# A transformer-like pair of blocks on one core: the first projections read the input before its norm, and matmuls await the low part of their weights by quarters

## The chip, the cores and the metric

The kernel runs on one core of a Trainium2 chip, all in float32. The metric is the device time of one execution in microseconds (us), the median of several runs. TensorE is called PE here, VectorE DVE, ScalarE ACT, GpSimd POOL and SyncE SP, as in the profile.

## The reference, cut to what matters

Only the beginning of the first block matters for the first half of the change.

```python
def rms_norm(x, g):
    y = x * lax.rsqrt(jnp.mean(x * x, axis=-1, keepdims=True) + EPS)
    return y * g
...
h = rms_norm(x, mix_norm_g[l])              # x: 1024 tokens x 1024 channels
p = jnp.einsum("btd,de->bte", h, w_in[l])
(gm_u, gm_v, cv_a, cv_g, dn_q, dn_k, dn_v, dn_g, dn_beta, dn_alpha) = jnp.split(p, offsets, axis=-1)
y_a = spatial_gating(jax.nn.gelu(gm_u), jax.nn.gelu(gm_v), ...)   # gm_u, gm_v: 256 channels each
```

The factor `rsqrt(mean(x*x) + EPS)` belongs to a token, not to a channel. So it can also be multiplied into the result of the projection. After this come a convolution branch, a gated delta rule, an output projection, a SwiGLU (`ffn0`), and a second block (`ffn1`, attention with a state-space part and a gated linear unit `glu`, `ffn2`), each with its norms.

## The kernel before, in words

Activations lie transposed: 128 channels on the partitions, tokens along the free dimension, so `x[:, k, :]` is the k-th of 8 groups of channels. The 1024 tokens are worked on as two chunks of 512 columns, c = 0 and c = 1.

Each float32 product is three matmuls on rounded halves: both operands are split into a high part (`w_hi`, `h_hi`, rounded to the type `fp32r`) and a low part (`w_lo`, `h_lo`, the rest), and hi·hi, hi·lo and lo·hi are summed in a PSUM bank of `acc`. For the weights this goes as a pipeline over *slabs*. A slab is one output tile of 128 channels with all its k-tiles (`kt`, mostly 8). SP loads it to `w_raw[:, j]`, ACT copies it rounded to `w_hi[:, j]` (`w_high`), POOL subtracts to get `w_lo[:, j]` in four pieces of a quarter each (`split`, L558; each adds 1 to `split_done`), and PE runs `pe_slab`: 3 matmuls for each k and chunk, so 24 for a chunk of 8 k-tiles. There are two buffers, j = 0 and j = 1, and 368 slabs in all; a *pair* is one of each. SP reloads a `w_raw` buffer when its four pieces are done; ACT overwrites `w_hi[:, j]` when PE has finished the slab before in that buffer.

`slab_plan` lists the slabs as segments (`gm`, `cv`, `dn_kv`, ...). The first pair or so of a segment is written out, the others run in a hardware loop (`pe.Fori`), in which the number that a semaphore is compared with is computed in a register. Some segments are marked `fine`: in their written-out slabs PE awaits the quarter of `w_lo` that the next k needs. All other slabs, those in loops among them, await all four pieces before their first matmul (L675).

At the start ACT squares `x` (L622), PE sums the squares over the channels with a matrix of 1/1024 (L605, 16 matmuls of full float32), ACT takes the root (L627), DVE the reciprocal (L651), and DVE, ACT and POOL make `h = x*g*rs` and its halves (L661, L632, L665, L593), first for chunk 0 and then for chunk 1. PE begins with the 8 small outputs `logits` (L1155 to L1157) and the first pair of `gm` for chunk 0, and does the same for chunk 1. ACT applies Gelu from the bank to `gm_u` and `gm_v` (L1406, L1429). Then come the `cv` slabs. The order on each engine is that of the code.

Of the kernel before, what the change touches and what calls it, by code (L numbers as in the profile page):

```python
# [132 lines left out]
def slab_plan(t):  # L133
# [62 lines left out]
    add("gm", 2, KD, CH1, run(t["w_in"], 0))  # L196
# [84 lines left out]
def build_program(nc, t):  # L281
    with ExitStack() as ctx:
# [54 lines left out]
        sqx = place("sqx", W + 8 * col, [P, 2, L])  # L337
# [149 lines left out]

        @block.sync
# [60 lines left out]
        def _(pool):  # L549

            for name, seg in LOADED.items():
# [9 lines left out]
                if name not in ("gm", "out1a"):  # L561
# [6 lines left out]
                if name == "out1a":  # L568
                    pool.wait_ge(sem("x_kept"), 32)
                    pool.memset(xn[0:DB, :, DB:2 * DB], 0.0).then_inc(sem("xn_zero"), 1)  # L570
                    def mix_low(k, src):
                        pool.wait_ge(sem("mix_hi"), k + 1)
                        pool.tensor_tensor(h_lo[:, k, META:L], src, h_hi[:, k, META:L].bitcast(F32), ALU.subtract).then_inc(sem("o_lo"), 1)

                    for k in range(2):
                        mix_low(k, gm_u2[:, k, :])
                    for p in range(2):
                        pool.wait_ge(sem("o_scaled"), 2 * p + 2)
                        for hd in range(HEADS):
# [10 lines left out]
                for c, (c0, w) in enumerate(seg.chunks):  # L590
                    for k in POOL_LO if name == "gm" else ():
                        pool.wait_ge(sem("hi_mix1"), c * KD + k + 1)
                        pool.tensor_tensor(h_lo[:, k, c0:c0 + w], tmp[:, k % 4, 0:w], h_hi[:, k, c0:c0 + w].bitcast(F32),  # L593
                                           ALU.subtract).then_inc(sem("lo_written"), 1)
# [5 lines left out]
        def pe_first_norm(pe):  # L600

            for c, (c0, w) in enumerate(CH1):
                for k in range(KD):
                    pe.wait_ge(sem("sqt_mix1"), c * KD + k + 1)
                    ins = pe.matmul(acc[:, c, 0:w], const("mean"), sqx[:, k % 2, c0:c0 + w],  # L605
                                    start=(k == 0), stop=(k == KD - 1), skip_group_check=True)
                    ins.then_inc(sem("sqsum_mix1"), 1)

        def act_first_norm(act):

            for g in range(4):
                c, k = g // 2, 4 * (g % 2)
                c0, w = CH1[c]
                act.dma_start(x[:, k:k + 4, c0:c0 + w], t["x"][:, k:k + 4, c0 - META:c0 - META + w]).then_inc(sem(f"x_full{g}"), 16)

            def square(c, k):
                c0, w = CH1[c]
                if k % 4 == 0:
                    act.wait_ge(sem(f"x_full{2 * c + k // 4}"), 16)
                if k >= 2:  # L620
                    act.wait_ge(sem("sqsum_mix1"), c * KD + k - 1)
                act.activation(sqx[:, k % 2, c0:c0 + w], x[:, k, c0:c0 + w], ACT.Square).then_inc(sem("sqt_mix1"), 1)  # L622

            def root(c):
                c0, w = CH1[c]
                act.wait_ge(sem("sqsum_mix1"), (c + 1) * KD)
                act.activation(rs[:, c0:c0 + w], acc[:, c, 0:w], ACT.Sqrt, bias=const("eps")).then_inc(sem("sd_mix1"), 1)  # L627

            def high(c, k):
                c0, w = CH1[c]  # L630
                act.wait_ge(sem("scaled_mix1"), c * KD + k + 1)
                act.copy(h_hi[:, k, c0:c0 + w], tmp[:, k % 4, 0:w]).then_inc(sem("hi_mix1"), 1)  # L632

            act.wait_ge(sem("params_full"), 32)
            for k in range(KD):
                square(0, k)
            root(0)
            for j in range(2):
# [8 lines left out]
        def dve_norm(dve, own, name, chunks, gain):

            for c, (c0, w) in enumerate(chunks):
                dve.wait_ge(sem("sd_" + name), c + 1)  # L650
                own.link(dve.reciprocal(rs[:, c0:c0 + w], rs[:, c0:c0 + w]))  # L651
                for k in range(KD + 2):
                    if k < KD:
                        g = c * KD + k
                        if g >= 4:
                            before = (k - 4) % KD
                            if before in POOL_LO:
                                dve.wait_ge(sem("lo_written"), (g - 4) // KD * len(POOL_LO) + POOL_LO.index(before) + 1)
                            else:
                                own.wait()  # L660
                        dve.scalar_tensor_tensor(tmp[:, k % 4, 0:w], x[:, k, c0:c0 + w], gain[:, k:k + 1],  # L661
                                                 rs[:, c0:c0 + w], ALU.mult, ALU.mult).then_inc(sem("scaled_" + name), 1)
                    if k >= 2 and k - 2 not in POOL_LO:
                        dve.wait_ge(sem("hi_" + name), c * KD + k - 1)
                        own.mark(dve.tensor_tensor(h_lo[:, k - 2, c0:c0 + w], tmp[:, (k - 2) % 4, 0:w],  # L665
                                                   h_hi[:, k - 2, c0:c0 + w].bitcast(F32), ALU.subtract))
                own.wait()
                dve.sem_inc(sem("h_written"), 1)

        def pe_slab(pe, seg, i, j, rhs, only=None, late=None):  # L670

            n = len(seg.chunks)
            fine = seg.fine and isinstance(i, int) and only is None
            if not fine:
                pe.wait_ge(split_done, i * (2 * LOW_PIECES) + LOW_PIECES * (seg.n0 + j + 1))  # L675
            for c, (c0, w) in enumerate(seg.chunks):
# [7 lines left out]
                for k in range(seg.kt):  # L684
# [5 lines left out]
                    rh, rl = rhs[0][:, k, c0:c0 + w], rhs[1][:, k, c0:c0 + w]  # L690
# [191 lines left out]

        def pe_first_pair(pe, seg, beside):

            for c in range(len(seg.chunks)):
                h_ready(pe, c)
                beside(c)
                for j in range(2):
                    pe_slab(pe, seg, 0, j, (h_hi, h_lo), only=c)
# [254 lines left out]
        def pe_mix1(pe):  # L1144
            h = (h_hi, h_lo)

            def logits_chunk(c):

                if c == 0:
                    pe.wait_ge(sem("ba_full"), 1)  # L1150
                name = f"logits_{c}"
                aux_take(pe, name)
                out, cols = aux(name)[0:8, :], slice(META + 512 * c, META + 512 * (c + 1))
                for k in range(KD):
                    pe.matmul(out, ba_hi[:, k, :], h_hi[:, k, cols], start=(k == 0), stop=False)  # L1155
# [11 lines left out]
            for j in range(2):  # L1167
                pe_slab(pe, SEG["gm"], 1, j, h)
# [231 lines left out]
        def act_mix1(act):  # L1400
# [3 lines left out]
            def first_pair(j, c):  # L1404
# [1258 lines left out]
```

## Time and profile before

| | us |
|---|---|
| median of 3 runs | 3679.59 (3678.3 to 3680.5) |
| the profiled execution, its own time | 3681.67 |
| its span (first to last instruction) | 3679.9 |
| PE busy | 3562.0 (97%) |
| DVE, ACT, POOL busy | 1440.2, 958.7, 1129.1 |
| mean granted TensorE clock | 0.985 |

The span is what the trace covers; the own time is 1.8 us more. The durations below come from this execution, the forecast is made against the median, 2.1 us below its own time. A clock of 1.00 is TensorE's higher level, 2.4 GHz, and 0.50 the lower, 1.2 GHz.

### The profile page before, as it was taken

To read this page: it belongs to the slowest core of one execution; us is meant where nothing else is said; L and a number is where in the kernel's file an instruction comes from. 1 tells how busy PE (TensorE), PEld (TensorE's weight loads), DVE (VectorE), ACT (ScalarE), POOL (GpSimd) and SP (SyncE) were. 2 spreads that over 40 slices of the span, in tenths; PEclk is the share of its full clock that TensorE was granted. 3 is DMA by queue.
4 is the path that set the end of the run, shared out by engine and by line. 5 is a ranking of instruction groups with operands and counts; after the bars stand their busy time and mean duration, and the time that the engine had idled before them with its cause. 6 is when DMAs were issued, how large, how long until landed. Compare 5 with 4: busy or idle time off the path is not lost.

```text
span 3679.9 us, 52405 instructions
## 1 busy us (share of the span) xinstructions
PE 3562.0 (97%) x20104; PEld 2947.3 (80%) x20104; DVE 1440.2 (39%) x2514; ACT 958.7 (26%) x1678; POOL 1129.1 (31%) x1503
## 2 busy tenths in 40 slices
PE   7998889999999999999999989999999999999998
PEld 4787777888888878899999878887777788888886
DVE  3297455211111163412122473836876521111214
ACT  4244443111111142111111233115653321111112
POOL 3242135322222253222222442301015532222223
PEclk9999899999999999999999999999999999999999
DMA  2111112111111121111111232111024221111112
GB/s 99 47 46 41 51 69 86 60 49 46 46 49 48 42 79 56 42 46 43 49 42 54 59 123 86 35 36 38 30 90 143 86 68 47 46 46 52 46 44 99
DMA packets 79299, 217.45 MB, mean 59 GB/s; under 512 B 18848, under 2 KB 18976, under 8 KB 78496
## 3 DMA queue, kind: packets, MB, share of 16 engines
q1 hardware_dynamic: 60960, 171.25, 15.1%
q10 hardware_dynamic: 18176, 43.93, 3.3%
q8 instruction: 114, 1.87, 0.2%
q14 instruction: 49, 0.40, 0.0%
HBM read 194.62 MB, written 19.46 MB: 58 GB/s over the span
## 4 chain that ended last, share of the span: by engine, by line
issue 61%; POOL 24%; PE 11%; DVE 2%; ACT 1%; DMA 1%; POOLq 1%; SPq 0%; ACTq 0%; DVEq 0%
POOL w_lo L558 23%; PE acc L691 2%; PE acc L692 2%; PE acc L693 2%; PE acc L1225 0%; POOLq L562 0%; DVE cv_acc L1700 0%; PE acc L1220 0%; DVE acc L1778 0%; DVE x_up L1781 0%; PE acc L605 0%; PE acc L1339 0%; DMA x<-in_x_dram 0%; PE acc L1282 0%; PE acc L1312 0%
## 5 line engine op out<-in xcount | busy, mean ns | idle before, releaser
L558 POOL TENSOR_TENSOR w_lo<-w_raw,w_hi 128x256 fp32r<-128x256 f32 (+3 forms) x1472 | 1090.3, 773 | 2415.4 <-ACT w_hi L528 2415.1
L691 PE MATMUL acc<-h_hi,w_hi 128*128 128x512 f32 (+1 forms) x3552 | 1318.4, 371 | 27.5 <-POOL w_lo L558 19.9
L692 PE MATMUL acc<-h_lo,w_hi 128*128 128x512 f32 (+1 forms) x3552 | 1317.3, 371 | 0.0
L693 PE MATMUL acc<-h_hi,w_lo 128*128 128x512 f32 (+1 forms) x3552 | 1311.8, 369 | 0.0
L691 PEld LDWEIGHTS acc<-h_hi,w_hi 128*128 128x128 f32 x3552 | 672.2, 189 | 156.6 <-issue 20.5
L692 PEld LDWEIGHTS acc<-h_lo,w_hi 128*128 128x128 f32 x3552 | 671.4, 189 | 120.0 <-issue 1.9
L693 PEld LDWEIGHTS acc<-h_hi,w_lo 128*128 128x128 f32 x3552 | 672.3, 189 | 117.0
L528 ACT CAST w_hi<-w_raw 128x1024 fp32r<-128x1024 f32 (+3 forms) x368 | 344.1, 936 | 1242.4 <-PE acc L693 1230.7
L971 DVE TENSOR_TENSOR ff_hi<-tmp,acc 128x512 f32 (+3 forms) x154 | 94.5, 614 | 1100.5 <-PE acc L693 1065.0
L691 PE MATMUL acc<-ff_hi,w_hi 128*128 128x512 f32 (+1 forms) x1232 | 449.4, 365 | 5.4 <-POOL w_lo L558 2.9
L693 PE MATMUL acc<-ff_hi,w_lo 128*128 128x512 f32 (+1 forms) x1232 | 447.1, 363 | 0.0
L692 PE MATMUL acc<-ff_lo,w_hi 128*128 128x512 f32 (+1 forms) x1232 | 446.6, 362 | 0.0
L1009 DVE SCALAR_TENSOR_TENSOR x<-acc,x 128x512 f32 (+1 forms) x168 | 103.3, 617 | 440.8 <-PE acc L693 439.6
L691 PEld LDWEIGHTS acc<-ff_hi,w_hi 128*128 128x128 f32 x1232 | 231.8, 188 | 52.3 <-issue 6.7
L693 PEld LDWEIGHTS acc<-ff_hi,w_lo 128*128 128x128 f32 x1232 | 231.6, 188 | 38.0
L692 PEld LDWEIGHTS acc<-ff_lo,w_hi 128*128 128x128 f32 x1232 | 231.3, 188 | 38.2 <-issue 0.7
L938 ACT ACTIVATE tmp<-acc 128x512 f32<-128x512 f32 (+1 forms) x136 | 72.9, 537 | 532.8 <-PE acc L693 532.6
L976 DVE TENSOR_TENSOR ff_lo<-tmp,ff_hi 128x512 f32 (+3 forms) x154 | 113.9, 740 | 23.0 <-DVE tmp L973 20.7
L842 DVE SCALAR_TENSOR_TENSOR x<-acc,x 128x512 f32<-128x512 f32 (+1 forms) x88 | 56.6, 643 | 165.4 <-PE acc L693 160.2
L973 DVE TENSOR_TENSOR tmp<-tmp,acc 128x512 f32<-128x512 f32 (+1 forms) x154 | 93.4, 606 | 0.0
L1700 DVE SCALAR_TENSOR_TENSOR cv_acc<-cv_y,params,cv_acc 128x1024 f32<-128x1024 f32 x60 | 80.5, 1388 | 0.0
L2257 ACT ACTIVATE sc<-sc,st 128x272 f32<-128x272 f32 (+1 forms) x128 | 64.0, 500 | 32.1 <-DVE st L2504 29.1
(361 smaller groups left out, 2978.0 us busy)
## 6 DMA issues: line engine op xcount, KB each, us to landing
w_raw<-in_ffn_w_dram SPq DMA_DIRECT2D x94, 512.0 KB, 3.5
w_raw<-in_w_in_dram SPq DMA_DIRECT2D x58, 512.0 KB, 3.5
w_raw<-in_w_out_dram SPq DMA_DIRECT2D x32, 512.0 KB, 3.5
w_raw<-in_ffn_w_dram SPq DMA_DIRECT2D x48, 320.0 KB, 2.9
w_raw<-in_w_gate_dram SPq DMA_DIRECT2D x24, 512.0 KB, 3.5
w_raw<-in_w_up_dram SPq DMA_DIRECT2D x24, 512.0 KB, 3.5
w_raw<-in_ffn_w_dram SPq DMA_DIRECT2D x32, 384.0 KB, 3.0
gates_kept<-gstage ACTq DMA_DIRECT2D x32, 256.0 KB, 2.0
```

Of the source, the lines that this page charges most:

```text
L528: act.copy(w_hi[:, j, 0:width], w_raw[:, j, 0:width]).then_inc(sem("w_high"), 1)
L558: pool.tensor_tensor(w_lo[:, j, a:a + step], w_raw[:, j, a:a + step], w_hi[:, j, a:a + step].bitcast(F32), ALU.subtract).then_inc(split_do ...
L691: pe.matmul(bank, wh, rh, start=(k == 0), stop=False)
L692: pe.matmul(bank, wh, rl, start=False, stop=False)
L693: ins = pe.matmul(bank, wl, rh, start=False, stop=(k == seg.kt - 1))
L938: act.activation(tmp[:, c, 0:w], acc[:, c, 0:w], ACT.Silu).then_inc(acc_free[0], 1)
L971: own.mark(dve.tensor_tensor(hi, g, up, ALU.mult))
L973: dve.tensor_tensor(tmp[:, 3:4, 0:w], g, up, ALU.mult).then_inc(acc_free[1], 1)
L976: own.mark(dve.tensor_tensor(ff_lo[:, bass.ds(f, 1), c0:c0 + w], tmp[:, 3:4, 0:w], hi.bitcast(F32), ALU.subtract))
L1009: dve.scalar_tensor_tensor(xt, acc[:, 3 * j + c:3 * j + c + 1, 0:w], scale, xt, ALU.mult, ALU.add).then_inc(acc_free[j], 1)
L1700: own.mark(dve.scalar_tensor_tensor(cv_acc[:, ct, :], src, w, cv_acc[:, ct, :], ALU.mult, ALU.add))
L2257: own.mark(act.activation(probs(u, hd), probs(u, hd), ACT.Exp, bias=st[0:nq, b, 0, hd:hd + 1], accum_out=st[0:nq, b, 1, hd:hd + 1]))
```

## The change

1. The slabs of `gm` are cut up in another way. `gm_a` is both pairs for chunk 0, on `hx = x*g` without the norm's factor. `gm_r` runs the second pair again for chunk 1 with the weights that are still there, and `gm_b` loads the first pair again for chunk 1, both on `h` with the norm. So two more slabs are loaded and split, and no matmul of theirs is done twice.
2. `hx` gets its own halves in tiles of its own (`hx_hi` by ACT, `hx_lo` by DVE). PE's 16 float32 matmuls for the sum of squares become one for each chunk, since DVE first adds the squares of the 8 k (`ssq0`). DVE multiplies the results of `gm_a` and of `logits` for chunk 0 by the factor `rs0`, and Gelu is then applied in place. All low parts of `h` are made by DVE and none by POOL, first for chunk 1, then for chunk 0.
3. `x` comes in six transfers and not four: parts of 0.5 MB on SP's and ACT's queues for chunk 0, then two of 1 MB. The constants are loaded behind the first weights.
4. `pe_slab` awaits quarters of `w_lo` in every slab, in loops too, except where it runs for one chunk alone (`only`).

```diff
-    add("gm", 2, KD, CH1, run(t["w_in"], 0))
+    add("gm_a", 2, KD, CH1[:1], run(t["w_in"], 0), lambda i, j, c: 3 * j + i)
+    add("gm_r", 1, KD, CH1[1:], None, lambda i, j, c: 3 * j + 2, again=True)
+    add("gm_b", 1, KD, CH1[1:], run(t["w_in"], 0), lambda i, j, c: 3 * j)
...
+        X_PARTS = [(0, 0, 2), (0, 2, 2), (0, 4, 2), (0, 6, 2), (1, 0, 4), (1, 4, 4)]
...
-            sp.dma_start(consts[:, :], t["consts"]).then_inc(sem("params_full"), 16)
             sp.dma_start(params[:, :], t["params"]).then_inc(sem("params_full"), 16)
...
                     for j in range(2):
+                        load_x(sp, 2 * j)
                         load(0, j)
+                    sp.dma_start(consts[:, :], t["consts"]).then_inc(sem("consts_full"), 16)
...
+        def pe_first_mean(pe, c):
+            pe.wait_ge(sem("x_added"), (KD - 1) * (c + 1))
+            pe.matmul(acc[:, 6 + c, :], const("mean"), ssq0[:, c, :], start=True, stop=True, skip_group_check=True)\
+              .then_inc(sem("x_ms"), 1)
...
+            for g in (1, 3, 4, 5):
+                load_x(act, g)
...
+            for k in range(KD):
+                raw_high(k)
+                if k % 4 == 3:
+                    w_high(act, SEG["gm_a"], 0, k // 4)
             for k in range(KD):
                 square(0, k)
+            w_after(act, SEG["gm_a"], 0, 0)
             for k in range(KD):
                 square(1, k)
+            act.wait_ge(sem("consts_full"), 16)
+            w_after(act, SEG["gm_a"], 0, 1)
+            for c in range(2):
+                root(c)
             for k in range(KD):
+                act_first_high(act, 1, k)
...
+        def dve_first_norm(dve, own):
+            for k in range(KD):
+                dve.wait_ge(sem("hx_hi_full"), k + 1)
+                dve.scalar_tensor_tensor(hx_lo[:, k, :], x[:, k, FIRST], gain[:, k:k + 1], hx_hi[:, k, :].bitcast(F32),
+                                         ALU.mult, ALU.subtract).then_inc(sem("hx_full"), 1)
+            for c in range(2):
+                for k in range(1, KD):
...
+                    dve.tensor_tensor(ssq0[:, c, :], ssq0[:, c, :], sq0[:, n % 3, :], ALU.add).then_inc(sem("x_added"), 1)
+            for c in range(2):
+                dve.wait_ge(sem("sd_mix1"), c + 1)
+                own.mark(dve.reciprocal(rs0[:, c, :], rs0[:, c, :]))
...
+            split(1)
+            for i in range(2):
+                for j in range(2):
+                    acc_wait(dve, SEG["gm_a"], i, j, 0)
+                    dve.tensor_tensor((gm_u, gm_v)[i][:, j, 0:512], acc[:, 3 * j + i, :], rs0[:, 0, :], ALU.mult).then_inc(acc_free[j], 1)
...
+            split(0)
...
-            fine = seg.fine and isinstance(i, int) and only is None
+            fine = only is None
...
+            pe_slab(pe, gm_a, 0, 0, hx, late=lambda c, k: pe.wait_ge(sem("hx_full"), k + 1), at=META)
+            pe_slab(pe, gm_a, 0, 1, hx, at=META)
+            pe.wait_ge(sem("consts_full"), 16)
+            pe_first_mean(pe, 0)
+            pe_slab(pe, gm_a, 1, 0, hx, late=lambda c, k: pe_first_mean(pe, 1) if k == 6 else None, at=META)
+            pe_slab(pe, gm_a, 1, 1, hx, at=META)
+            logits_chunk(0, hx, META)
+            pe_slab(pe, gm_r, 0, 0, h, late=lambda c, k: pe.wait_ge(sem("lo_mix1"), k + 1))
+            logits_chunk(1, h, 0)
+            pe_slab(pe, gm_r, 0, 1, h)
+            pe_slab(pe, gm_b, 0, 0, h)
...
-            for j in range(2):
-                pe_slab(pe, SEG["gm"], 1, j, h)
+            pe_slab(pe, gm_b, 0, 1, h)
+            pe.wait_ge(sem("lo_mix1"), 2 * KD)
             pe_slab(pe, SEG["cv"], 0, 0, h)
```

Here is how PE's own order begins. Before, the sums of squares stand ahead of the first product (`sqx` are the squares, `ba_hi` the weights of `logits`):

```order
L605 MATMUL acc<-sqx,consts 128x512 [waits sqt_mix1,params_full]
L605 MATMUL acc<-sqx,consts 128x512 [waits sqt_mix1] x15
```

After the change, PE's order begins with the first slab, which waits for a piece of `w_lo` and for one k of `hx_lo`:

```order
L725 MATMUL acc<-hx_hi,w_hi 128x512 [waits split_done,hx_full]
L726 MATMUL acc<-hx_lo,w_hi 128x512
L727 MATMUL acc<-hx_hi,w_lo 128x512
L725 MATMUL acc<-hx_hi,w_hi 128x512 [waits hx_full]
L726 MATMUL acc<-hx_lo,w_hi 128x512
L727 MATMUL acc<-hx_hi,w_lo 128x512
L725 MATMUL acc<-hx_hi,w_hi 128x512 [waits split_done,hx_full]
```

The 16 matmuls on squares have left PE's front, and weights stand there.

DVE's order after the change, behind the eight `hx_lo` (L667): the sums, both reciprocals, and the first splits of chunk 1, which PE's `gm_r` slab awaits one by one (`ssq_77`, `sq_75` and `rs_76` are `ssq0`, `sq0` and `rs0`):

```order
L667 SCALAR_TENSOR_TENSOR hx_lo<-x,params,hx_hi 128x512 [waits hx_hi_full] x7
L675 TENSOR_TENSOR ssq_77<-ssq_77,sq_75 128x512 [waits x_sq]
L675 TENSOR_TENSOR ssq_77<-ssq_77,sq_75 128x512 [waits x_added,x_sq] x13
L678 RECIPROCAL rs_76<-rs_76 128x512 [waits sd_mix1] x2
L687 SCALAR_TENSOR_TENSOR gm_u<-x,params,rs_76 128x512 [waits dve_own]
L687 SCALAR_TENSOR_TENSOR gm_u<-x,params,rs_76 128x512
L687 SCALAR_TENSOR_TENSOR gm_v<-x,params,rs_76 128x512
L691 TENSOR_TENSOR h_lo<-gm_u,h_hi 128x512 [waits hi_mix1]
```

Before, DVE had one reciprocal and then the splits of chunk 0, and POOL made most of the low parts; now both reciprocals stand ahead of the first split.

In a loop body (`ffn0`'s up projections, and all others alike) PE had this at the head of its first slab:

```order
L700 UNCONDITIONAL_BRANCH
L700 ISA
L680 ISA [waits split_done]
L691 MATMUL acc<-h_hi,w_hi 128x512 [waits acc_free0]
L692 MATMUL acc<-h_lo,w_hi 128x512
L693 MATMUL acc<-h_hi,w_lo 128x512
```

Now it has a register operation and a wait more for each further quarter:

```order
L722 ISA [waits acc_free0]
L725 MATMUL acc<-h_hi,w_hi 128x512 [waits split_done]
L726 MATMUL acc<-h_lo,w_hi 128x512
L727 MATMUL acc<-h_hi,w_lo 128x512
L725 MATMUL acc<-h_hi,w_hi 128x512
L726 MATMUL acc<-h_lo,w_hi 128x512
L727 MATMUL acc<-h_hi,w_lo 128x512
L722 REGISTER_ALU
L725 MATMUL acc<-h_hi,w_hi 128x512 [waits split_done]
```

The wait for the whole split has become one for its first piece, and three register operations with a wait each have come into each slab of a loop.

## Rows read from the trace of the kernel before

**Rows 1.** Whom PE waited for, over the span: total, times, longest.

```profile
PE acc L691 <- POOL w_lo L558: 25.7, 17, 5.3
PE acc L605 <- ACT sqx L622: 21.2, 5, 12.9
PE acc L1225 <- DVE dec_s L1721: 10.3, 4, 4.7
```

**Rows 2.** Busy time (instructions) of PE, PEld, DVE, ACT, POOL by stretch; PEclk, DMA share, GB/s.

```profile
16.00:42.00 26.00, 17.27 (x29) 5.16 (x27) 14.69 (x11) 16.44 (x26) 15.64 (x14) 0.84 0.23 74
42.00:99.50 57.50, 57.44 (x250) 41.28 (x251) 16.65 (x17) 22.14 (x33) 18.27 (x18) 0.98 0.13 42
```

**Rows 3.** Timeline of the first stage: start, duration, engine, line, operation.

```profile
0.76 6.65 ACTq L614 DMA_DIRECT2D x<-in_x_dram  x4
8.24 0.20 DVE L2594 CAST ba_hi<-params 128x64 fp32r<-128x64 f32 x1 [8.24 <-DMA params<-in_params_dram]
10.82 1.28 ACT L622 ACT_TABLE_LOAD   x1 [10.82 <-DMA x<-in_x_dram]
12.11 1.15 ACT L622 ACTIVATE sqx<-x 128x512 f32<-128x512 f32 x2
22.89 1.98 ACT L528 CAST w_hi<-w_raw 128x1024 fp32r<-128x1024 f32 x2
42.31 3.35 DVE L651 RECIPROCAL rs<-rs 128x512 f32<-128x512 f32 x1 [2.71 <-ACT rs L627]
99.46 0.60 ACT L1429 ACTIVATE gm_v<-acc 128x512 f32<-128x512 f32 x1 [4.96 <-PE acc L693]
```

**Rows 4.** Lines L661, L558, L665 in the first 60 us: ns min/median/max.

```profile
L661 DVE SCALAR_TENSOR_TENSOR tmp<-x,params,rs x16: 739/1061/1789, 26.4 to 55.2; 128x512 f32<-128x512 f32 x16
L558 POOL TENSOR_TENSOR w_lo<-w_raw,w_hi x8: 724/950/1180, 24.0 to 30.1; 128x256 fp32r<-128x256 f32 x8
L665 DVE TENSOR_TENSOR h_lo<-tmp,h_hi x4: 678/1218/1779, 34.2 to 55.8; 128x512 fp32r<-128x512 f32 x4
```

**Rows 5.** Lines near to the operations that are new, over the span.

```profile
L1686 DVE TENSOR_TENSOR gm_u<-gm_u,acc x4: 686/688/689, 164.1 to 170.2; 128x512 f32<-128x512 f32 x4
L712 PE MATMUL acc<-ssq,consts x22: 385/592/1061, 570.2 to 3666.0; 128*128 128x512 f32 x18, 128*128 128x264 f32 x4
```

**Rows 6.** Timeline behind the first stage, with what DVE's idle time was ended by.

```profile
114.40 0.43 DVE L1663 BATCH_NORM_STATS2 small<-gm_t 128x6 f32<-128x256 f32 x1 [28.47 <-ACT gm_t L1445]
```

**Rows 7.** PE at the first slab of `at_g`, and POOL's pieces for this pair.

```profile
2180.93 9.09 POOL L558 TENSOR_TENSOR w_lo<-w_raw,w_hi 128x256 fp32r<-128x256 f32 x8 [9.11 <-ACT w_hi L528]
2185.53 0.79 PE L691 MATMUL acc<-h_hi,w_hi 128*128 128x512 f32 x1 [3.58 <-POOL w_lo L558]
```

**Rows 8.** PE alone by stretch: busy (instructions), PEclk, DMA share, GB/s.

```profile
2185.50:2191.00 5.50, 5.47 (x13) 0.51 0.29 95
```

**Rows 9.** Whom PE waited for in the loop of `glu`, 2744 to 2830 us.

```profile
PE acc L691 <- POOL w_lo L558: 2.9, 3, 1.5
```

**Rows 10.** Timeline at a turn of that loop.

```profile
2746.97 0.39 PE L693 MATMUL acc<-y_hi,w_lo 128*128 128x512 f32 x1
2748.81 0.49 PE L691 MATMUL acc<-y_hi,w_hi 128*128 128x512 f32 x1 [1.46 <-POOL w_lo L558]
...
2751.46 0.39 PE L693 MATMUL acc<-y_hi,w_lo 128*128 128x512 f32 x1
2751.69 0.40 PE L691 MATMUL acc<-y_hi,w_hi 128*128 128x512 f32 x1
...
2754.47 0.40 PE L691 MATMUL acc<-y_hi,w_hi 128*128 128x512 f32 x1
```

**Rows 11.** PE's sequencer in loops: register operations and waits, ns min/median/max.

```profile
L680 PEldq ALU_OP  x109: 32/36/42, 707.0 to 3584.6; - x109
L680 PEldq EVENT_SEMAPHORE  x84: 51/51/51, 712.6 to 3590.3; - x84
```

**Rows 12.** Line L675 between 2748 and 2752 us: its register operation.

```profile
L675 PEldq ALU_OP  x1: 32/32/32, 2750.3 to 2750.3; - x1
```

More of the change, by code:

```diff
@@ L590, in _ @@
[L590 to L594, printed above, removed]
+                pool.wait_ge(sem("x_kept"), 32)
+                pool.memset(xn[0:DB, :, DB:2 * DB], 0.0).then_inc(sem("xn_zero"), 1)
@@ L597, in _, with first_stage @@
                         split(i, j)
[L600 to L607, printed above, removed]
-        def act_first_norm(act):
[L611 to L614, printed above, removed]
+        def first_stage(c, k):
+            return (gm_u, gm_v)[k % 4 // 2][:, k % 2, 512:1024] if c else tmp0[:, k % 4, :]
@@ L647, in dve_norm, with act_first_high @@
[L647 to L651, printed above, removed]
+                act_first_high(act, 1, k)
+        def act_first_high(act, c, k):
+            c0, w = CH1[c]
+            act.wait_ge(sem("scaled_mix1"), first_no(c, k) + 1)
+            act.copy(h_hi[:, k, c0:c0 + w], first_stage(c, k)).then_inc(sem("hi_mix1"), 1)
@@ L663, in dve_norm @@
[L663 to L670, printed above, removed]
+                        if k >= 4:
+                            dve.wait_ge(sem("lo_mix1"), first_no(c, k) - 3)
@@ L1402, in act_mix1, with second_gelu @@
             act.dma_start(gm_par[:, :], t["gm"]).then_inc(sem("gm_par_full"), 16)
-            def first_pair(j, c):
-                acc_wait(act, SEG["gm"], 0, j, c)
-                act.activation(gm_u[:, j, cc(c)], acc[:, 3 * j + c, :], ACT.Gelu).then_inc(acc_free[j], 1)
-            for c in range(2):
-                aux_wait(act, f"logits_{c}")
-                aux_release(act.copy(lgt[0:8, cc(c)], aux(f"logits_{c}")[0:8, :]), f"logits_{c}")
-                for j in range(2):
-                    if c:
-                        w_after(act, SEG["gm"], 0, j)
-                    first_pair(j, c)
+            def second_gelu(seg, tile, j):
+                acc_wait(act, seg, 0, j, 0)
+                act.activation(tile[:, j, 512:1024], acc[:, seg.bank(0, j, 0), :], ACT.Gelu).then_inc(acc_free[j], 1)
+            for i in range(2):
+                for j in range(2):
+                    act.wait_ge(acc_free[j], chunk_no(SEG["gm_a"], i, 0) + 1)
+                    dst = (gm_u, gm_v)[i][:, j, 0:512]
+                    own.mark(act.activation(dst, dst, ACT.Gelu))
+            for k in range(KD):
+                act_first_high(act, 0, k)
+                if k == 3:
+                    w_high(act, SEG["gm_b"], 0, 0)
+                    second_gelu(SEG["gm_r"], gm_v, 0)
+            aux_wait(act, "logits_1")
+            aux_release(act.copy(lgt[0:8, cc(1)], aux("logits_1")[0:8, :]), "logits_1")
+            second_gelu(SEG["gm_r"], gm_v, 1)
+            w_high(act, SEG["gm_b"], 0, 1)
+            own.wait()
+            for j in range(2):
+                act.wait_ge(acc_free[j], chunk_no(SEG["gm_r"], 0, 0) + 1)
+            act.sem_inc(sem("gm_full"), 8)
+            second_gelu(SEG["gm_b"], gm_u, 0)
+            w_after(act, SEG["gm_b"], 0, 0)
             aux_wait(act, "logits")
@@ L1425, in act_mix1 @@
             act.sem_inc(sem("z_ln_full"), 1)
-            for j in range(2):
-                for c in range(2):
-                    acc_wait(act, SEG["gm"], 1, j, c)
-                    act.activation(gm_v[:, j, cc(c)], acc[:, 3 * j + c, :], ACT.Gelu).then_inc(acc_free[j], 1)
-                w_after(act, SEG["gm"], 1, j)
-            for j in range(2):
-                act.wait_ge(acc_free[j], chunk_no(SEG["gm"], 1, 1) + 1)
-            act.sem_inc(sem("gm_full"), 8)
+            second_gelu(SEG["gm_b"], gm_u, 1)
+            w_after(act, SEG["gm_b"], 0, 1)
             for s in range(4):
```

142 lines of the change are left out of this document (70 added, 72 removed).

## The prediction, made before the kernel was run

> **What bounds the kernel now.** I first asked the page's table of busy times: PE works for 97% of the span, so a gain can only come out of the 3% in which it stands still, out of matmuls that go away, or out of a higher clock. Next came the list of whom PE waits for [rows 1]. It shows 21.2 us for the squares of the first norm, 25.7 us in 17 waits for the first low weights, and 10.3 us for DVE in the delta rule. Then I went to the places. At the start PE has 29 records in 16 to 42 us, halves of the full float32 sums, then 250 in 57.44 us at 0.230 us each, without a gap [rows 2]. The stage ends when ACT reads `gm_v`, at 99.46 [rows 3]. So the start is 42 us of preparation and 57.4 us of products. In the later pairs I looked at two kinds of wait for `w_lo`: at `at_g`, 3.58 us [rows 7], and in the loop of `glu`, 2.9 us in three [rows 9].
>
> **The start, step by step.** Removed: the norm of chunk 0 stands no longer ahead of the first product. What must still be there is `x`, its gain, and a piece of weights.
> - ACT's own queue issues `x` until 0.76 + 6.65 = 7.4; the table load of 1.28 follows, 8.7 [rows 3]. Before, ACT waited until 10.82, when its 1 MB part landed. Now the first part is 0.5 MB, on SP's queue behind parameters that landed at 8.24 even behind the constants, which now come later. So `x` is no longer last here, ACT's issue is.
> - Four casts to `hx_hi`, priced as squares of the same shape, 1.15 / 2 = 0.575 each: 11.0. Half a slab of `w_hi`, 1.98 / 2 = 0.99: 12.0 [rows 3]. POOL's first piece at its fastest, 0.72 [rows 4]: **PE begins at 12.7**, not at 42.0.
> - The products are the same 240, and 10 small ones, so 57.4 us if fed; two sums over channels take 0.6 each [rows 5]: 12.7 + 57.4 + 1.2 = 71.3.
> - PE then starts from rest. At `at_g`, 13 matmuls after a wait took 5.47 us at a granted clock of 0.51 [rows 8], the lower of the two levels, 2.5 more than 13 x 0.23. The old stretch has a clock of 0.98 over 57.5 us [rows 2], so about 1.2 of this is in it already: 1.3 more, 72.6. This also covers `hx_lo`, which DVE makes at 0.74 to 1.06 each [rows 4] while a k takes PE 3 x 0.42.
> - The critical hand-off is `gm_r`. PE has 120 matmuls ahead of it (four slabs and `logits`): 12.7 + 27.6 + 1.2 + 2.5 = 44.0. DVE must by then have done 8 `hx_lo`, 14 additions, two reciprocals and the first splits. The additions follow ACT's squares (8 x 0.575 for each chunk between casts of weights), and end at about 23 and 29. The second sum stands in PE's third slab at k = 6, at about 30.7; with a root behind it the reciprocals run from 31.4 to 38.1, 3.35 each [rows 3]. Three scalings go ahead of the first low part: 38.1 + 3 x 0.74 + 0.68 = 41.0, the next each 1.42 later [rows 4]. PE wants one each 0.69 from 44.0 on. The first five are early; k = 5 is there at 48.1 and wanted at 47.5, and the last two need no scaling, 48.8 and 49.5. That makes 0.6 of waiting; I take 0.9 with what a late root would add: **`cv` starts at 73.5, a gain of 26.0**.
> - Behind it: four products from the bank, 0.69 each [rows 5], to 52.3; then the split of chunk 0, 11.3 us undisturbed, 18.2 at the medians [rows 4], to 63.6 or 70.5. `cv` wants it at 73.5. It is hidden, with 3 us left at worst. The two further slabs cost ACT 2 us and POOL four pieces each (2.9 to 4.7) [rows 3, 4]. The first is wanted at 60.6 and its buffer is free at 49.5; the second is wanted at 66 and its buffer is free at 60.6, and by quarters it is 61.6 + 0.7 to 1.2. Both are hidden; with no cover each would cost 5 to 7.
> - The two ends: with no stall of any kind 71.3, a gain of 28.2. If DVE ran split and scalings at medians, 2.28 a pair for 1.42, the split of chunk 1 costs 6.9 more, and a reciprocal or root late by 1 adds to it: gain 18. I am near the good end, because POOL has nothing to split between 35 and 49: `gm_r` uses weights that are there, and the next slab's buffer is still held.
>
> DVE operations with both inputs in SBUF spread from 0.68 to 1.78 us here while POOL's pieces spread from 0.72 to 1.18 [rows 4], but the product that reads PSUM stays within 0.686 to 0.689 [rows 5]. The Trainium skill, GpSimd page ("Specifications"), states that GpSimd shares its SBUF interfaces with VectorE and contends with instructions of two SBUF inputs; by that rule alone a DVE chain beside four slabs of splitting would run at its medians and the gain be near 18, and by the rows, since POOL rests at that time, 26.
>
> **Does it last?** The later chain shifts with it if nothing there is tied to something other than PE. DVE is idle for 28.47 us before 114.40, waiting for ACT's Gelu behind PE's bank [rows 6], so it can go 26 earlier. Loads have room: the DMA share is 0.13 in the dense stretch [rows 2].
>
> **The quarter waits.** Most of the 25.7 us [rows 1] are in slabs that are already `fine` and wait for their first piece. The others can be recovered:
> - `at_g`: POOL makes 8 pieces in 9.09 us from 2180.93, 1.14 each [rows 7], and PE begins at 2185.53, after four. With one it could begin at 2182.1, 3.4 earlier. It then runs through pieces that arrive each 1.14, for 6 matmuls of both chunks each; at the lower clock they take 6 x 0.42 = 2.5, so nothing is late. Part of the clock's start-up now lies in time that was idle: of 2.5 I take 1.0. Sum 4.4.
> - `glu`: 1.5 + 0.7 + 0.7, seen at a turn of the loop as 2748.81 after 2746.97 where the chain border is 0.23 [rows 9, 10]. A first quarter is there some 2 to 3 us before the fourth, so all 2.9 go, and the 0.49 for 0.40 that the restart costs: 3.4 with two more such.
> - Together 7.8; other such slabs, 0.2: 8.0. Ends: 0 if the first piece too is late by as much, 12 if the clock's start-up goes altogether in both.
>
> Added: 84 loop bodies with two slabs of three more quarters, 504 register operations and waits, 0.032 and 0.051 us on the sequencer [rows 11]. What hides them: the sequencer passes the register operation of the second slab at 2750.3 [rows 12], PE's matmul behind it starts at 2754.47 [rows 10], so it is 4.2 us ahead. Where such operations already stand at a chunk border, the pitch is 0.23 [rows 10]. I take 0. Without the lead they would cost 504 x 0.083 = 42 us. Behind each wait PE's whole queue stands; pieces come in order, one each 1.2 at most against 6 matmuls of 1.39, so each later piece has been made when its turn comes.
>
> **Sum.** Own time 3681.7 - 26.0 - 8.0 = 3647.7. The profiled execution is 2.1 above the median, so 3645.6; I say **3646**.
>
> **Rivals.** A measurement can tell about 0.2%, 7.4 us.
> 1. The forecast, 3641 to 3652: **0.60**.
> 2. DVE late at `gm_r`: gain at the start of 16 to 20 and not 26, 3652 to 3656, with 3 more if `cv` waits for the split of chunk 0. For it: a slack of nothing from k = 5 on, and spreads up to 1.79 us [rows 4]. Against: POOL is idle then. **0.20**.
> 3. The quarter waits recover nothing, as the first piece comes as late: about 3653. Against: four pieces before 2185.53 from 2180.93 [rows 7]. **0.05**.
> 4. PE, fed by a k at a time, stays at the lower level through the four slabs of `gm_a`: about 100 matmuls x 0.19 = 19 us more, 3665. Before, in a stretch with 8.7 us of gaps in 26, the clock was 0.84 [rows 2], which speaks against it. **0.04**. The Trainium skill, "TensorE: Matmul & The Clock Gate" ("HAM oscillation"), tells of a kernel whose short bursts between waits each began throttled; by it each thinly fed slab would go at the lower level.
> 5. The start's gain is given back in a later stage that DVE bounds (the third row of [rows 1]), about 3672, no change. Against: DVE's 28 us of idle time. **0.04**.
> 6. Slower: the waits are not hidden. A matmul that follows a wait would be sent only when the sequencer has passed operation and wait, each of the 504 showing as 0.083: +42 - 34 = about 3688. It decides from 34 / 504 = 0.067 each. For it: the lead was read at one place, and quarters come 6 matmuls apart. Against: the lead itself and the pitch of 0.23. **0.04**.
> 7. Better: the clock's start-up vanishes in more places and the start loses nothing, about 3636. **0.03**.
>
> The range 3640 to 3659 takes in cases 1 to 3 and leaves 4 to 7, 0.15, outside. Faster by over 0.2%: cases 1 to 4 and 7, **0.92**; within: case 5, **0.04**; slower: case 6, **0.04**.
>
> **What would show it.** In the new profile: the first product at 12.7 (right if 12 to 14); the first `cv` matmul at 73.5 and its waits for `lo_mix1` under 1.5; DVE's split of chunk 1 at 0.74 and 0.68 an operation; reciprocals from about 31.4; no wait for `w_lo` over 1 us at `at_g`, and none in `glu`; 0.23 from matmul to matmul over a quarter border in loops; later stages each 26 earlier. It is wrong if the clock in 13 to 40 us is nearer to 0.5 than to 0.9, if PE waits for DVE before 50 by over 5 us, or if gaps of 0.03 to 0.1 stand at quarter borders.

## The result, and the profile after

| | before | after |
|---|---|---|
| median of 4 runs, us | 3678.95 (3676.68 to 3680.50) | 3645.20 (3639.88 to 3652.62) |
| ratio, 95% interval | | 0.9906 (0.9893 to 0.9918) |
| span of the profiled execution | 3679.9 | 3642.3 |
| PE busy | 3562.0 | 3532.6 |
| mean granted TensorE clock | 0.985 | 0.990 |

The change takes off 0.94%, 33.75 us by the medians. The forecast was 3646 with a gain of 34.0. The profiled execution of the changed kernel is one of its quicker ones: the spans of the two profiled executions differ by 37.6.

First the start. This is the timeline of the changed kernel, answering to [rows 3] (start, duration, engine, line, operation).

```profile
0.76 2.55 ACTq L501 DMA_DIRECT2D x<-in_x_dram  x4
7.45 1.28 ACT L624 ACT_TABLE_LOAD   x1 [7.45 <-DMA x<-in_x_dram]
13.19 0.77 PE L725 MATMUL acc<-hx_hi,w_hi 128*128 128x512 f32 x1 [13.19 <-POOL w_lo L567]
13.75 0.63 PE L726 MATMUL acc<-hx_lo,w_hi 128*128 128x512 f32 x1
32.51 6.56 DVE L678 RECIPROCAL rs<-rs 128x512 f32<-128x512 f32 x2 [0.67 <-ACT rs L637]
63.15 0.47 PE L725 MATMUL acc<-h_hi,w_hi 128*128 128x512 f32 x1 [1.07 <-POOL w_lo L567]
75.19 0.40 PE L725 MATMUL acc<-h_hi,w_hi 128*128 128x512 f32 x1
80.95 0.59 ACT L1496 COPY cv_a<-acc 128x512 f32<-128x512 f32 x1 [1.04 <-PE acc L727]
```

PE's first product stands at 13.19 and the first of `cv` at 75.19. In the old trace ACT read the first `cv_a` at 105.02, now at 80.95: the start gives 24.1. In the same trace by stretches (PE's busy time and number of matmuls, then granted clock, DMA share, GB/s), answering to [rows 2]:

```profile
13.10:18.90 5.80, 5.71 (x14) 1.00 1.01 388
18.90:75.00 56.10, 55.03 (x240) 1.00 0.23 68
```

The first 14 matmuls take 5.71 / 14 = 0.41 each, the pace of the lower level, as at `at_g` before [rows 8], although the clock's column says 1.00 there. All others take 55.03 / 240 = 0.229. The only wait in 62 us is the one of 1.07 at 63.15.

Second the quarters. Whom PE waits for over the span (total, times, longest), answering to [rows 1]; 13.2 of the first row is the program's beginning, so 20.1 are left of the 25.7 before:

```profile
PE acc L725 <- POOL w_lo L567: 33.3, 15, 13.2
PE acc L1261 <- DVE dec_s L1764: 10.4, 5, 4.7
PE acc L1300 <- DMA xn<-gates_kept: 7.8, 1, 7.8
PE acc L725 <- POOL h_lo L581: 4.4, 1, 4.4
```

At `at_g`, where [rows 7] had a wait of 3.58, PE's timeline goes on without one:

```profile
2156.44 0.23 PE L2054 MATMUL acc<-ssm_in,bl 128*32 128x32 f32 x3
2156.69 0.47 PE L725 MATMUL acc<-h_hi,w_hi 128*128 128x512 f32 x1
2157.00 0.39 PE L726 MATMUL acc<-h_lo,w_hi 128*128 128x512 f32 x1
2157.23 0.39 PE L727 MATMUL acc<-h_hi,w_lo 128*128 128x512 f32 x1
```

The matmul pitch is 0.23 from the second on, where it was 0.42 [rows 8]. At the turn of the `glu` loop of [rows 10]:

```profile
2716.31 0.39 PE L727 MATMUL acc<-y_hi,w_lo 128*128 128x512 f32 x1
2716.54 0.40 PE L725 MATMUL acc<-y_hi,w_hi 128*128 128x512 f32 x1
```

Its list of waits for 2699 to 2799 us has no `w_lo` any more (before: [rows 9]):

```profile
PE acc L725 <- DVE y_lo L2570: 0.6, 3, 0.2
PE acc L725 <- DVE q L2565: 0.4, 1, 0.4
```

Laying equal instructions of the two traces beside each other, the lead of the new kernel over the old goes like this: 24.1 when `cv` begins; 22.8 at the first inverse (L1300), where PE waits 7.8 for a transfer and before waited 5.35; 27.4 at `out1`, after stretches in which the old kernel met the lower clock more often; 25.3 just ahead of `at_g`, 31.3 behind it; 30.7 at `glu`, 35.4 behind it; 36.8 by 2944 of the old trace; 37.6 at the end. So `at_g` gives 6.0 and `glu` 4.7.

### The profile page after: what moved, and what is told of

It is laid out like the page before. It is cut to its first block, busy times and chain, and to the rows that moved or that the text cites. A ratio compares the mean times of both kernels' runs of the same rounds, so it can differ in the third digit from the quotient of the medians.

```text
span 3642.3 us, 52856 instructions
## 1 busy us (share of the span) xinstructions
PE 3532.6 (97%) x20076; PEld 2933.7 (81%) x20076; DVE 1462.0 (40%) x2553; ACT 964.8 (26%) x1687; POOL 1124.6 (31%) x1499
## 4 chain that ended last, share of the span: by engine, by line
issue 61%; POOL 24%; PE 9%; DVE 4%; ACT 1%; DMA 1%; POOLq 1%; SPq 0%; ACTq 0%; DVEq 0%
POOL w_lo L567 24%; PE acc L725 2%; PE acc L726 2%; PE acc L727 2%; DVE cv_acc L1743 1%; POOLq L571 0%; PE acc L1261 0%; DVE acc L1821 0%; PE acc L1256 0%; DVE ssq L675 0%; DVE x_up L1824 0%; PE acc L1392 0%; PE acc L1348 0%; PE acc L1384 0%; DVE cvo L1783 0%
## 5 line engine op out<-in xcount | busy, mean ns | idle before, releaser
L567 POOL TENSOR_TENSOR w_lo<-w_raw,w_hi 128x256 fp32r<-128x256 f32 (+3 forms) x1480 | 1103.9, 777 | 2394.7 <-ACT w_hi L537 2394.2
L725 PE MATMUL acc<-h_hi,w_hi 128*128 128x512 f32 (+1 forms) x3520 | 1304.2, 371 | 27.0 <-POOL w_lo L567 17.2
L726 PE MATMUL acc<-h_lo,w_hi 128*128 128x512 f32 (+1 forms) x3520 | 1302.8, 370 | 0.0
L727 PE MATMUL acc<-h_hi,w_lo 128*128 128x512 f32 (+1 forms) x3520 | 1297.2, 369 | 0.0
L725 PEld LDWEIGHTS acc<-h_hi,w_hi 128*128 128x128 f32 x3520 | 664.6, 189 | 155.2 <-issue 21.8
L726 PEld LDWEIGHTS acc<-h_lo,w_hi 128*128 128x128 f32 x3520 | 664.0, 189 | 118.3 <-issue 1.9
L727 PEld LDWEIGHTS acc<-h_hi,w_lo 128*128 128x128 f32 x3520 | 665.0, 189 | 115.3
L726 PE MATMUL acc<-ff_lo,w_hi 128*128 128x512 f32 (+1 forms) x1232 | 447.2, 363 | 0.0
L726 PEld LDWEIGHTS acc<-ff_lo,w_hi 128*128 128x128 f32 x1232 | 232.0, 188 | 38.2 <-issue 0.7
```

What stands on the lines that cost most here:

```text
L567: pool.tensor_tensor(w_lo[:, j, a:a + step], w_raw[:, j, a:a + step], w_hi[:, j, a:a + step].bitcast(F32), ALU.subtract).then_inc(split_do ...
L725: pe.matmul(bank, wh, rh, start=(k == 0), stop=False)
L726: pe.matmul(bank, wh, rl, start=False, stop=False)
L727: ins = pe.matmul(bank, wl, rh, start=False, stop=(k == seg.kt - 1))
```

## The experiments

**e1, the start alone.** The quarter waits are taken back, except in `gm_a` and `gm_b`.

```diff
-            fine = only is None
+            fine = seg.fine and isinstance(i, int) and only is None
```

> The changed kernel with the quarter waits taken back: loops and the written-out slabs that had them not before await all four pieces of w_lo again, gm_a and gm_b keep quarters. Theory (the two halves of the change are worth 24 and 8 us and don't touch each other): 3679 - 24 = 3655, first product at 13.2, the cv slabs 24.1 earlier than before, and the waits of 3.6 at at_g and 2.9 in glu are back. Rival (the start's gain is partly given back later and the quarters carry the sum): 3660 or more. Rival (the quarters are worth nothing, what looked like their gain is the clock's luck): 3645.

Measured: 3654.05 (3650.23 to 3655.55), ratio 0.9939 (0.9925 to 0.9953). PE's waits are back where they were, at `at_g` in the timeline:

```profile
2156.80 0.79 PE L725 MATMUL acc<-h_hi,w_hi 128*128 128x512 f32 x1 [3.54 <-POOL w_lo L567]
```

and for `glu` in its list of waits, 2690 to 2790 us:

```profile
PE acc L725 <- POOL w_lo L567: 3.6, 4, 1.5
```

Its ACT reads the first `cv_a` at 80.84. The start is worth 0.61%, 22.4 us by the ratio and 24.1 by the medians.

**e2, the quarters alone.** The same line edited the other way in the kernel before.

> The kernel before with the quarter waits alone, in every slab that is not run for one chunk. Theory: 3679 - 8 = 3671, at_g without its wait and without its stretch at the lower clock (5.6 us together in the profile after), glu without its waits (4.7). Rival (waits in loops cost something that the start's gain covers): 3679 or more. Rival (each added wait unhidden, 0.083 us): 3713.

Measured: 3671.70 (3667.14 to 3676.24), ratio 0.9981 (0.9972 to 0.9990), so 3.7 to 10.3 us. PE's waits for `w_lo` (before: 25.7 in 17):

```profile
PE acc L691 <- POOL w_lo L558: 18.1, 12, 4.5
```

The two halves add up: 0.61% and 0.19% make 0.80%, the whole is 0.94%, within the intervals. No added wait in a loop made the kernel slower, and the start's gain covers no loss.

**e3, more waits.** The changed kernel with two further waits for each slab, on things long done.

```diff
                         pe.wait_ge(split_done, LOW_PIECES * (i * 2 + seg.n0 + j) + seg.low_pieces(k))
+                        if seg.low_pieces(k) == 2:
+                            pe.wait_ge(raw_full[j], (i + seg.n0 // 2 + 1) * 16)
+                        if seg.low_pieces(k) == 3:
+                            pe.wait_ge(sem('w_high'), i * 2 + (seg.n0 + j + 1))
```

> The changed kernel with two more waits in each slab, on semaphores that are satisfied long before (the load of the raw weights at the second quarter, the rounding of the high part at the third). In loops each is one more operation on PE's sequencer, 336 in all, beside registers. Theory (the sequencer runs some 4 us ahead, so such operations are hidden): 3645, no change, pitch over a quarter border 0.23. Rival (they show, 0.05 to 0.083 each): 3662 to 3673.

Measured: 3643.06 (3640.00 to 3648.47), ratio 0.9911 (0.9896 to 0.9926). PE's sequencer shows the added operations (ns min/median/max):

```profile
L724 PEldq EVENT_SEMAPHORE  x260: 51/51/1071, 13.3 to 3620.8; - x130
L724 PEldq FUSED_REGOPS  x84: 37/37/42, 674.8 to 3542.7; - x84
L726 PEldq EVENT_SEMAPHORE  x176: 51/51/5808, 14.5 to 3621.2; - x176
L726 PEldq ALU_OP  x168: 32/32/32, 676.2 to 3555.2; - x168
```

In the same trace's timeline the matmul pitch in a loop of `glu` stays 0.23:

```profile
2715.33 0.40 PE L729 MATMUL acc<-y_hi,w_hi 128*128 128x512 f32 x1
2715.56 0.40 PE L730 MATMUL acc<-y_lo,w_hi 128*128 128x512 f32 x1
```

Of these 688 operations 336 stand in loops: 84 register operations and 84 waits on L724, and 168 register operations on L726. The other 352 are waits in slabs that are written out. By their medians those in loops alone are 12.8 us of the sequencer, and all of them 30.7; the time did not rise. Waits that are satisfied cost PE nothing here, and the rival that had the change slower is out.

**e4, the old loads.** The changed kernel with `x` in four transfers of 1 MB on ACT's queue, and constants and parameters first on SP's.

```diff
-        X_PARTS = [(0, 0, 2), (0, 2, 2), (0, 4, 2), (0, 6, 2), (1, 0, 4), (1, 4, 4)]
+        X_PARTS = [(0, 0, 4), (0, 4, 4), (1, 0, 4), (1, 4, 4)]
...
-                        load_x(sp, 2 * j)
...
-            for g in (1, 3, 4, 5):
+            for g in range(4):
```

> The changed kernel with the loads of before: x in four parts of 1 MB all on ACT's queue, constants and parameters first on SP's. Theory (the first cast waits for data): ACT's table load begins at 10.8 and not at 7.5, the first product at 16.5 and not at 13.2, and the cv slabs are 3.3 later, 3648. Rival (the hand-off to gm_r, which DVE feeds, decides, and has slack): less than 1 us later at cv.

Measured: 3648.33 (3643.73 to 3651.35), ratio 0.9925 (0.9909 to 0.9941). The trace is sharper than the time:

```profile
10.88 1.28 ACT L623 ACT_TABLE_LOAD   x1 [10.88 <-DMA x<-in_x_dram]
16.63 0.76 PE L724 MATMUL acc<-hx_hi,w_hi 128*128 128x512 f32 x1 [16.63 <-POOL w_lo L566]
```

First product 3.44 later, first `cv_a` at 84.35, 3.40 later. So of the start's 24.1 the new loads (smaller parts of `x` on two queues, the constants later; the edit takes both back together) carry 3.4, and the work that is taken from ahead of the products the other 20.7.

**e5, DVE late.** A third reciprocal of 3.35 us ahead of the first split.

```diff
             own.wait()
+            own.mark(dve.reciprocal(gm_u[:, 0, 0:512], rs0[:, 1, :]))
+            own.wait()
```

> The changed kernel with a third reciprocal of 3.35 us on DVE ahead of the first split, its result unused. In the trace after, the low part of k = 7 for gm_r is done at 49.3 and PE comes to it at about 50.0, so DVE has 0.7 us in hand. Theory (this hand-off decides beyond that slack): PE waits about 2.6 in gm_r, the POOL piece of gm_b moves with DVE, cv 2.6 to 3.4 later, about 3648. Rival (there is slack elsewhere that takes it up): PE without a wait before 60, cv not later by 1.

Measured: 3648.03 (3645.73 to 3650.27), ratio 0.9917 (0.9900 to 0.9934). PE in `gm_r`, and its wait at `gm_b`:

```profile
46.25 0.50 PE L727 MATMUL acc<-h_hi,w_hi 128*128 128x512 f32 x1 [0.30 <-DVE h_lo L693]
66.29 0.47 PE L727 MATMUL acc<-h_hi,w_hi 128*128 128x512 f32 x1 [1.55 <-POOL w_lo L567]
```

Five such steps go at DVE's pace, 1.265, and not at PE's 0.695: 2.85 later, with the longer wait at `gm_b` 3.1 by the first `cv_a` (84.05). In the changed kernel PE had no wait in `gm_r` at all. DVE's first low part came 3.14 later than there (44.24 for 41.10) and cost 2.85, so the slack is 0.3 by this; the changed kernel's trace has the last low part done at 49.3 and PE at it at 50.1, 0.8. The hand-off that rival 2 named is real and was met by little.

**e6, POOL first.** At 57 us POOL's piece for `gm_b` takes 5.77 and not 0.72. The timeline of the changed kernel shows it with DVE's operations of two SBUF inputs, one behind the other until 62.42:

```profile
57.23 5.77 POOL L567 TENSOR_TENSOR w_lo<-w_raw,w_hi 128x256 fp32r<-128x256 f32 x1 [23.42 <-ACT w_hi L537]
57.34 0.73 DVE L687 SCALAR_TENSOR_TENSOR tmp<-x,params,rs 128x512 f32<-128x512 f32 x1
58.01 0.67 DVE L691 TENSOR_TENSOR h_lo<-tmp,h_hi 128x512 fp32r<-128x512 f32 x1
60.54 1.88 DVE L691 TENSOR_TENSOR h_lo<-tmp,h_hi 128x512 fp32r<-128x512 f32 x3
```

The edit lets DVE pause:

```diff
                 for k in range(KD + 2):
+                    if c == 0 and k == 6:
+                        dve.wait_ge(split_done, LOW_PIECES * (SEG["gm_b"].n0 + 1))
```

> The changed kernel, in which DVE pauses in the split of chunk 0 (ahead of its seventh scaling) until POOL has the four pieces of gm_b's first slab. In the trace after, POOL's first piece there takes 5.77 us, exactly as long as DVE runs operations with two inputs in SBUF without a pause, and PE waits 1.07. Theory (DVE starves POOL): the piece takes 0.73, PE's wait at 63.15 goes, cv 1.1 earlier, the split of chunk 0 ends 3 us later, still ahead of cv; time 1 less, hard to tell by itself. Rival (the piece is long for a reason of POOL's own, as code that is loaded): it stays at 5 to 6, DVE then stands as long, and cv is later.

Measured: 3644.00 (3642.83 to 3651.61), ratio 0.9910 (0.9893 to 0.9926). POOL and DVE in its trace:

```profile
57.32 2.05 POOL L567 TENSOR_TENSOR w_lo<-w_raw,w_hi 128x256 fp32r<-128x256 f32 x1 [23.43 <-ACT w_hi L537]
58.09 0.67 DVE L693 TENSOR_TENSOR h_lo<-tmp,h_hi 128x512 fp32r<-128x512 f32 x1
61.49 0.75 DVE L689 SCALAR_TENSOR_TENSOR tmp<-x,params,rs 128x512 f32<-128x512 f32 x1 [2.73 <-POOL w_lo L567]
```

The piece ends 0.6 after DVE has stopped, 1.4 of its 2.05 us being DVE's, and PE has no wait between 40 and 80; first `cv_a` 79.70, 1.25 earlier. In all eight traces with the new start and without this pause the piece takes 5.77 or 5.78, in all three with it 2.05 or 2.06. So DVE held POOL off. The Trainium skill, "GPSIMD Engine Reference" ("Specifications"), says that GpSimd shares its SBUF interfaces with VectorE and contends with its instructions of two SBUF inputs; the trace agrees, and shows that such contention can be a stop for POOL and free for DVE (its operations stay at 0.73 and 0.67). It is not always so. In the changed kernel between 12 and 34 us both are slowed, DVE's `hx_lo` beside POOL's pieces from 0.74 to 1.22, and the pieces from 0.72 to 1.18 (lines L667 and L567, ns min/median/max):

```profile
L667 DVE SCALAR_TENSOR_TENSOR hx_lo<-x,params,hx_hi x8: 742/751/1223, 9.5 to 15.9; 128x512 fp32r<-128x512 f32 x8
L567 POOL TENSOR_TENSOR w_lo<-w_raw,w_hi x16: 724/1180/1231, 12.3 to 33.1; 128x256 fp32r<-128x256 f32 x16
```

The last four `hx_lo` followed each other without a gap too; what decides between sharing and a stop no run here shows.

The time did not follow: a gain of 1 is less than the runs can tell, and the clock moved as well. PE's busy time and matmuls, clock, DMA share and GB/s for 138.50 to 148.60 us, in the changed kernel and then in e6:

```profile
138.50:148.60 10.10, 10.10 (x90) 1.00 0.17 54
```

```profile
138.50:148.60 10.10, 10.10 (x61) 0.54 0.18 54
```

**e7, the first pieces.** Of the 20.1 us of waits left, most are for a first piece. At 599, 1345 and 2900 it is ACT that rounds the weights late.

```diff
             root(1)
+            first = not final and name != "mix2"
+            if first:
+                w_after(act, SEG[NEXT_SEG[segs[1].name]], 0, 0)
             for k in range(KD):
...
-                        w_after(act, early, i, j)
+                        if not (first and (i, j) == (0, 0)):
+                            w_after(act, early, i, j)
```

> The changed kernel; in the norms ahead of ffn0, ffn1 and ffn2 ACT rounds the weights of the second pair's first slab ahead of the first h_hi, in the 4.2 us in which it waits for DVE, and no longer behind the third. Theory (the first pieces were late only by ACT's order, which quarter waits can't mend): the waits of PE of 2.8, 3.1 and 2.8 at about 599, 1344 and 2900 go, 8.7 us and some of the clock's start-up, 3645 - 9 to 12 = 3634. Rival (the next thing, the low part of h, is late by as much): 3643 or more.

Measured: **3631.94** (3628.65 to 3634.16), ratio 0.9871 (0.9855 to 0.9888). PE's waits:

```profile
PE acc L725 <- POOL w_lo L567: 26.9, 14, 13.2
```

6.4 us of waiting are gone, a new one of 1.6 at 1343, for the second slab of the same pair, counted in. The clock was 0.992 for 0.990, some 4 us of the 13 by the slope given below; the other 2 to 3 I can't assign.

**e8, e9, e10, e11: the norm ahead of attention.** There the wait was the longest, 5.27. e8 has e6's and e7's edits, the rounding early there too, and the store of `x` (`when_read`, 4 MB) behind it; e9 is e8 without DVE's pause; e10 is e9 with the second slab's rounding early as well, where a norm has two such pairs (first two lines below); e11 is e10 with the pause.

```diff
-        TURN_W2 = {2: ((0, 0),), 5: ((0, 1),)}
+        TURN_W2 = {2: ((0, 0), (0, 1))}
...
-            first = not final and name != "mix2"
+            first = not final
```

> e6 and e7 together, e7's edit for the norm ahead of the attention block as well, and there the store of x (4 MB, 14.8 us, ahead of which the load of these weights took 12.1 instead of 3.6) is issued behind that rounding. Theory: the wait of 5.3 at 2117 goes as well: 3645 - 1 - 9 - 5 = 3630, with the clock 3626. Rival (the store then ends later, and its readers or the loads behind it make another wait): 3634 or more.

> e8 without DVE's pause for POOL. e8 was no faster than e7 (3632.7 and 3631.9), though its wait at 2117 fell from 5.3 to 1.6 and 1.3. Theory (the pause moves the start, and in e6 and e8 the conv stretch behind it then fell to the lower clock for 10.2 us at 139 to 149): without it 3632 - 2.3 = 3629.6. Rival (the late store of x costs what it gave, by waits of a kind that the list doesn't single out): 3632 or more.

> e9 in which ACT also rounds the second slab of that pair sooner, behind the third h_hi and not behind the sixth, where the norm has two such pairs (ahead of ffn1 and of the attention block). In e7 and e8 PE waits 1.6 there at 1343 and at 2117. Theory (again ACT's order alone): both go, 3.2 less than e9, 3626.5. Rival (the low part of h is then late, since its high parts stand behind the rounding): as e9.

> e10 with DVE's pause for POOL put in again, beside it on the same chip. Theory of the clock: no gain of the 1.1 that the first wait is worth, rather 1 to 4 slower than e10, and a long stretch at the lower clock at about 139. Rival (e6 and e8 met it by chance): 1 faster than e10.

Measured: e8 3632.70 (3628.87 to 3635.67), ratio 0.9870; e9 3632.39 (3628.90 to 3638.33), 0.9873; e10 3631.10 (3628.35 to 3633.93), 0.9867 (0.9850 to 0.9883); e11 3630.71 (3629.23 to 3635.57), 0.9865 (0.9848 to 0.9881). None can be told from e7. The forecasts of e8 to e10 (3630, 3629.6 and 3626.5) did not come about, and e9 and e10 lie where their rivals had them: the wait for `w_lo` at this place shrank and then went, and the time stayed. In the traces of e8 and e9 it is 1.63 and then 1.30 for 5.27, with 1.90 for 1.23 at L2053 some 24 us later. e10's list of PE's waits:

```profile
PE acc L725 <- POOL w_lo L567: 19.5, 10, 13.3
PE acc L725 <- issue: 4.9, 1, 4.9
```

The place in question in its timeline, on ACT and PE:

```profile
2119.02 0.21 ACT L2224 ACTIVATE small<-small 128x16 f32<-128x16 f32 x1 [0.26 <-DVEq L2404]
2119.51 2.06 ACT L2251 COPY u<-acc 128x264 f32<-128x264 f32 x4 [0.17 <-ACT small L2225]
2120.24 0.77 PE L725 MATMUL acc<-h_hi,w_hi 128*128 128x512 f32 x1 [4.88 <-issue]
```

No wait for `w_lo` stands there any more, and PE waits all the same, 4.88 for 5.27. Its sequencer stands in one operation all this time, which awaits the piece of `w_lo` and the bank together (line L722, 2112.5 to 2121 us, ns):

```profile
L722 PEldq EVENT_SEMAPHORE  x1: 7157/7157/7157, 2113.0 to 2113.0; - x1
```

It ends at 2120.18. POOL was done with this slab's four pieces at 2110.29, and ACT's first copy of `u` out of PE's banks ran from 2119.51 to 2120.14 and then freed a bank, so the bank is what came last. ACT came to that copy from a chain of small operations exchanged with DVE. From the last short wait for `w_lo` in the stage before (2101.74 in the changed kernel) to the first matmul of L2053 (L2049 in the changed kernel) it is 53.1 in the changed kernel, 51.7 in e9 and 53.3 in e10: what the first slab's rounding won there, the second's gave back. No run took the wait for the bank away.

e11 tells little of the pause. All three profiles of kernels with it (e6, e8, e11) have a stretch of 10.2 us at the lower clock from 138 or 139 on, and none of the eight others with the new start has one longer than 3.4 there. Yet e11's median is not above e10's. That the pause costs by the clock what it gives is neither borne out nor excluded by the times.

## Why the prediction was right

- **PE begins at 12.7.** 13.19. `x` was last after all (7.45, with ACT's issue done at 3.3), so my reason was wrong and its number near: the issue that took 6.65 before takes 2.55 now.
- **The start gains 26.0.** 24.1. The term that failed is "Both are hidden", of the two further slabs: POOL's piece took 5.77 where I bounded it at 1.2, and PE waited 1.07. The high part ahead of it was late as well, cast by ACT from 56.11 on though `gm_r` had left its buffer at 51; with a piece of 1.2 that alone would have been in time. I had weighed the shared interface for what POOL does to DVE, and not for what DVE does to POOL. At `gm_r` itself POOL rested, from 33.8 to 57.2, and DVE ran at 0.75 and 0.68 as the rows had it. The 0.9 for the hand-off was not needed, with reciprocals 1.1 later than I had them. The 1.2 taken off for a clock loss already in the old stretch should not have been, for its pitch of 57.44 / 250 = 0.230 is the 0.229 of the new one. The first product 0.5 late, these 1.2 and the wait of 1.07, less the 0.9, add 1.9 to 73.5: 75.4, where 75.2 is measured.
- **Quarters give 8.0.** At the two places the trace has 6.0 and 4.7, 10.7; by times e2 has 7 (3.7 to 10.3) and e1 against the whole 9. `at_g` was mis-sized at 4.4 and gave 6.0: I left 1.5 of the clock's start-up, but without the idle time before it PE did not fall to the lower level at all. `glu`, 3.4 in the forecast, gave 4.7; where the other 1.3 come from is not shown.
- **504 waits cost nothing.** So shown by e2 and e3. Unhidden they would have cost less than the 42 of the forecast, since such a wait in a loop is no operation of its own; the changed kernel's trace has 504 register operations for them, 16 us in all (ns):

```profile
L722 PEldq ALU_OP  x504: 32/32/42, 675.8 to 3557.5; - x168
```

- **It lasts.** Mostly: 24.1 at `cv` is 22.8 and 27.4 further on, 25.3 ahead of `at_g`. Two waits grew, 7.8 for 5.35 at the first inverse and 4.4 for 2.8 for POOL's `h_lo` at `out1`; the rest goes up and down, the clock with it. The first varies from 5.85 to 8.1 in the kernels with the new start, the second is 2.8 to 3.0 in most.
- **The sum.** A start 1.9 too high and quarters some 1 to 3 too low cancelled; part of the exactness is luck. By the traces 24.1, 6.0 and 4.7 make 34.8 of the 37.6; the other 2.8 stand at no one place. The four runs of the changed kernel spread over 12.7 us, and those of before over 3.8, though 15 further ones of it spread over 13.4. Over 57 runs of twelve kernels here (the changed one and e1 to e11), each kernel's runs taken about their own mean, the time is 2.2 us longer for each 0.001 that the mean clock is lower (correlation 0.84), so most of the spread goes with the clock.

Rival 1 holds. Rivals 3 (the quarters recover nothing) and 6 (the waits show) are excluded by e2 and e3. Rival 2 (DVE late at `gm_r`) did not come about, and e5 shows how near it was. Rival 4 (the lower level through `gm_a`) did not either: PE left that level after 14 matmuls, though fed by a k at a time. Nor did rival 5 (the gain is given back later): 24.1 are still there as 25.3 ahead of `at_g`. Rival 7's mechanism, start-ups that vanish, was there at `at_g`.

## What to carry to other kernels

A factor that belongs to the column of a result can be applied behind the product, and what it frees is all that stood ahead of the first product. Look then for the engine that gets the added work, for its slack was 0.3 to 0.8 us here. A wait by pieces for data that is made in pieces was free here, where the waiting engine's sequencer is ahead; it is worth the gap and the clock's start-up behind it. What is left after it is the first piece, and that was a matter of order on the engine that makes its input. Before mending such a wait, ask what PE would need next, since the longest of them hid another.

## What the runs showed of the hardware

A POOL operation of 0.72 us took 5.77 beside DVE operations of two SBUF inputs that followed each other without a pause, and ended 0.6 after their end; DVE lost nothing. Elsewhere in the same trace the same operation took 1.18 beside such a row of operations, and DVE's took 1.22 for 0.74. A wait that was already satisfied cost PE nothing: 688 more operations on its sequencer, 30.7 us by their own durations, left the time where it was. And a start shifted by 1.25 us went with another clock level 60 us later, in a stretch of small matmuls: 61 in 10.1 us for 90, a stretch of 10.2 us at the lower level in all three traces with that shift and in none of the eight without it.
